# The depthwise convolution's multiply moved from GpSimd to ScalarE in a one-core two-layer kernel

## What is computed

```python
u = a * jax.nn.sigmoid(ag)
u = jnp.pad(u, ((0, 0), (CONV_KSIZE - 1, 0), (0, 0)))
u = lax.conv_general_dilated(u, conv_w, (1,), 'VALID', dimension_numbers=('NWC', 'WIO', 'NWC'),
                             feature_group_count=CONV_WIDTH) + conv_b
u = jax.nn.silu(layer_norm(u, conv_ln_g, conv_ln_b))
```

## Time and profile before

| | |
|---|---|
| median of 3 runs | 2055.93 us (2053.12 to 2060.07) |
| profiled execution, its own time | 2055.43 us |
| its span | 2053.8 us |
| PE busy | 1906.3 us (93%) |
| DVE, ACT, POOL busy | 852.5, 585.5, 690.9 us |
| NSA units | from about 1270 to 1461 us of the span |

### The profile page before, as it was taken

The page is one execution under the profiler, slowest core; times in us unless marked ns, Lnnn a source line. Parts: engine busy times, 40 slices in busy tenths (PEclk is TensorE's granted clock), DMA queues, the critical chain, the costliest instruction groups (busy, mean ns, idle before and its releaser), DMA issues.

```text
span 2053.8 us, 23262 instructions
## 1 busy us (share of the span) xinstructions
PE 1906.3 (93%) x8758; PEld 1383.8 (67%) x8758; DVE 852.5 (42%) x1252; ACT 585.5 (29%) x1074; POOL 690.9 (34%) x396
## 2 busy tenths in 40 slices
PE   5999979999986899999779898999997989999999
PEld 3888757767866444444258776677675858888887
DVE  4221666645723122313253365667636643312331
ACT  2323334442221101110033223545444212222221
POOL 4444324332410000000022334776762424444442
PEclk9999989999995999999988999999998989999999
DMA  5222212242410577778832423121234412232231
GB/s 195 95 83 93 82 57 77 87 154 67 135 41 1 197 256 284 284 269 297 336 134 85 131 81 103 64 76 62 67 113 156 140 64 93 93 102 93 93 101 43
DMA packets 79301, 255.86 MB, mean 125 GB/s; under 512 B 8800, under 2 KB 9824, under 8 KB 79200
## 3 DMA queue, kind: packets, MB, share of 16 engines
q1 hardware_dynamic: 61632, 222.33, 31.5%
q10 hardware_dynamic: 17568, 32.11, 4.4%
HBM read 239.73 MB, written 14.68 MB: 124 GB/s over the span
## 4 chain that ended last, share of the span: by engine, by line
PE 85%; DVE 8%; DMA 3%; ACT 2%; issue 1%; ACTq 1%; SPq 0%; POOL 0%; DVEq 0%
PE psum L493 83%; DMA ring<-stream 2%; DVE root L1628 1%; DVE area_r L1610 1%; PE psum L1059 1%; DVE area L1617 1%; DVE area L1644 1%; DVE area L1697 1%; DVE root L1615 1%; ACTq L1547 1%; PE psum L584 1%; DVE area L2072 1%; ACT root L1191 1%; PE psum L749 0%; DMA area<-xT 0%
## 5 line engine op out<-in xcount | busy, mean ns | idle before, releaser
L493 PE MATMUL psum<-area_r,ring_hi 128*128 128x512 f32 (+1 forms) x3168 | 1004.4, 399 | 20.3 <-DVE area_r L1610 13.6
L413 POOL TENSOR_TENSOR ring_lo<-ring,ring_hi 128x1024 fp32r<-128x1024 f32 x220 | 533.0, 2426 | 1325.3 <-ACT ring_hi L1191 1325.3
L493 PEld LDWEIGHTS psum<-area_r,ring_hi 128*128 128x128 f32 x3168 | 596.1, 191 | 164.4 <-issue 26.4
L493 PE MATMUL psum<-area_r,ring_lo 128*128 128x512 f32 (+1 forms) x1584 | 622.3, 393 | 0.0
L1191 ACT ACTIVATE ring_hi<-ring 128x1024 fp32r<-128x1024 f32 x220 | 232.0, 1057 | 633.4 <-PE psum L493 604.6
L493 PEld LDWEIGHTS psum<-area_r,ring_lo 128*128 128x128 f32 x1584 | 302.9, 191 | 63.6
L493 PE MATMUL psum<-ring,area 128*64 128x512 f32 x768 | 195.4, 618 | 19.0 <-DMA ring<-stream 17.7
L1191 ACT ACTIVATE area<-psum 128x512 f32<-128x512 f32 (+3 forms) x248 | 119.8, 510 | 257.7 <-PE psum L493 143.4
L1628 DVE RECIPROCAL root<-root 128x512 f32<-128x512 f32 (+1 forms) x30 | 94.1, 3138 | 138.1 <-ACT root L1191 138.1
L493 PE MATMUL psum<-area 128*64 128x128 f32 (+6 forms) x832 | 112.1, 346 | 14.2 <-DVE area L1629 9.7
L493 PE MATMUL psum<-ring_hi,area_r 128*128 128x512 f32 (+1 forms) x352 | 107.6, 387 | 15.9 <-DVE area_r L1610 15.8
(11 more groups left out here) (193 smaller groups left out, 1641.9 us busy)
## 6 DMA issues: line engine op xcount, KB each, us to landing
ring<-stream SPq DMA_DIRECT2D x420, 512.0 KB, 3.5
area<-gates ACTq DMA_DIRECT2D x40, 256.0 KB, 5.9
gates<-root ACTq DMA_DIRECT2D x24, 256.0 KB, 2.0
gates<-area ACTq DMA_DIRECT2D x16, 256.0 KB, 3.5
area<-xT SPq DMA_DIRECT2D x8, 256.0 KB, 8.1
area<-xT ACTq DMA_DIRECT2D x8, 256.0 KB, 3.3
x_kept<-area ACTq DMA_DIRECT2D x8, 256.0 KB, 5.8
area<-x_kept ACTq DMA_DIRECT2D x8, 256.0 KB, 3.9
```

Of the source, the lines that this page charges most:

```text
L413: nc.gpsimd.tensor_tensor(ring_lo[:, c % RS, :], ring[:, c % R, :], ring_hi[:, c % RS, :].bitcast(F32), ALU.subtract).then_inc(w_lo, 1)
L493: return nc.tensor.matmul(out, lhsT, rhs, start=first, stop=last)
```

## The change

ScalarE makes the multiplies of GpSimd's 60 two-instruction steps, each as an activation `Copy` with the weight as a per-partition scale, into the same two scratch tiles. GpSimd keeps the add, and now takes four steps ahead of each `low`. In unit u ScalarE makes terms 4u+2 and 4u+3 between `gate2_out` and the four exponentials, and terms 4u+4 and 4u+5 behind the two small exponentials. Each term from the fifth step on first waits until GpSimd's add of step s-2, the last to read this scratch tile, is done.

```diff
@@ conv_step (GpSimd)
-                    term = tile(KVC + s % 2)
                     pool.wait_ge(S("conv_pool"), s - 1)
-                    link(nc.gpsimd.tensor_scalar(term, src, w, 0.0, ALU.mult, ALU.add))
-                    ins = nc.gpsimd.tensor_tensor(tile(CV + c), tile(CV + c), term, ALU.add)
+                    pool.wait_ge(S("conv_term"), s - 1)
+                    ins = nc.gpsimd.tensor_tensor(tile(CV + c), tile(CV + c), tile(KVC + s % 2), ALU.add)
                 ins.then_inc(S("conv_pool"), 1)
 
             for n in range(3 * KD):
-                for s in range(3 * n, min(3 * n + 3, 2 * TAPS)):
+                for s in range(4 * n, min(4 * n + 4, 2 * TAPS)):
                     conv_step(s)
@@ ScalarE
+            def conv_term(lo, hi):
+
+                for s in range(lo, min(hi, 2 * TAPS)):
+                    tap, c = divmod(s, 2)
+                    if s >= 4:
+                        act.wait_ge(S("conv_pool"), s - 1)
+                    A(tile(KVC + s % 2), upad[:, 2 + c, tap:tap + T], ACT.Copy, 0.0,
+                      par("convw", (2 + c) * TAPS + tap)).then_inc(S("conv_term"), 1)
@@ the loop over NSA units (ScalarE), behind gate2_out(u - 1), ahead of the four exponentials
                 if u < len(NSA_UNITS):
+                    if u == 0:
+                        act.wait_ge(S("conv_u"), CONVT)
+                        act.wait_ge(S("kv_xp"), 8)
+                    conv_term(2 + 4 * u, 4 + 4 * u)
                     n = P * (NSA_UNITS[u][1] + 1)
@@ the same loop, behind the two small exponentials
+                    conv_term(4 + 4 * u, 6 + 4 * u)
```

More of the change, by code:

```diff
@@ L238, in block_program @@
                      "vsw_out", "gn_mm", "gn_act", "kv_raw", "kv_x2", "kv_xp", "cmp_gelu", "cmp_mm", "cmp_out", "cmp_root",
-                     "conv_sig", "conv_out", "conv_pool", "on_rec", "on_bc", "on_norm", "ya_split", "conv_u", "ln_sum", "ln_d", "ln_sq", "ln_root", "ln_n", "ln_out",
+                     "conv_sig", "conv_out", "conv_pool", "conv_term", "on_rec", "on_bc", "on_norm", "ya_split", "conv_u", "ln_sum", "ln_d", "ln_sq", "ln_root", "ln_n", "ln_out",
                      "g2_in0", "g2_in1", "g2_in2", "g2_in3", "g2_act", "g2_out", "x3_out", "ff_silu", "ff_out", "fin", "xf_out", "br_split", "x_spilled", "g2_on", "stored"):
```

## The result

The changed kernel takes 2082.74 us (median of 4 runs, 2077.27 to 2088.63) against 2054.52 for the kernel before: a ratio of 1.0131, 95% interval 1.0105 to 1.0157. It is slower by 28.2 us between the medians; 2087 us was forecast from a base of 2055.9, that is 31 us more.

The account below looks back on a forecast made before the run. TensorE was taken to set the period; exponentials waiting for terms were to add 23.2 us and clock falls 7.8, together 31.0 on 2055.43 us: 2086.4, given as 2087 us. The range was 2066 to 2102 us.

Parts of the forecast that it names:

- Place and cause: Ahead of the exponentials, ScalarE's two front terms wait for GpSimd's adds behind low, delaying TensorE: +23.2 us.
- H: The end of a unit's ring_hi copy, where one NSA unit is cut from the next; GpSimd's low waits for it.
- One premise: In a unit, TensorE depends on fresh ScalarE work only at nsa_cscores, which needs the first two exponentials.
- C: The start of nsa_cscores in a unit; TensorE was said to have fixed work from there to the next H.
- The chain from H: In a unit: low, two GpSimd adds, signal and second term put the first exponential at H + 5.67 us.
- C minus H: Time from H to C in a unit: 6.53 to 7.17 us forecast by width, adding 23.2 us in all.
- VectorE's relief: GpSimd's shorter work leaves VectorE's L1697 and L1644 undisturbed; unit 15 gains 1.33 us, elsewhere exponentials wait for terms.
- "faster" rival: Relief counts, the wait doesn't: waits of 7.1 us and a 2.6 us clock fall go, 2046 us; chance 0.06.
- unit 2's wait: TensorE's 3.12 us wait in unit 2 before the change, laid to GpSimd holding up VectorE; the faster case removes it.
- The clock: TensorE's new waits halve its clock in units 1, 6, 10, 14, less unit 2's fall: 3 x 2.6 = 7.8 us.
- the middle terms: The two terms behind the small exponentials on ScalarE, forecast free in time; uncovered, up to 18 us in all.
- the stage: The stretch from C of unit 0 to C of unit 15, 176.2 us before the change and 204.1 after.

Follow-up runs that it names:

- e1_shift: Changed kernel, but GpSimd takes steps 4n+2 to 4n+5 ahead of each low (six ahead of the first); ratio 0.9986 against the kernel before.
- e2_four: Changed kernel with four scratch tiles for the terms instead of two, GpSimd's order kept; ratio 0.9999 against the kernel before.
- e6_one_column: Changed kernel with the two front terms of units 1 to 14 made for one column only, waits kept; one run, 2077.61 us.
- e3_behind: Changed kernel with the two front terms put behind the four exponentials; ratio 0.9979 against the kernel before.
- e4_no_terms: Changed kernel without ScalarE's terms and the waits for them, GpSimd keeping only its adds; ratio 0.9990 against the kernel before.
- e7_fill: Changed kernel with eight unused TensorE matmuls ahead of nsa_cscores in units 1, 2, 6, 10 and 14; ratio 1.0134 against the kernel before.
- e5_mul4: Kernel before the change with four GpSimd steps ahead of each low, multiplies left on GpSimd; ratio 1.0061 against the kernel before.

## Why the prediction held

- **Place and cause.** Right: the waits for GpSimd's steps 4u and 4u+1 behind `low`. e1_shift, e2_four and e6_one_column separate the wait from ScalarE's work: the exponentials start at H + 1.1 to 1.8 with the work and without the wait (e1_shift, from unit 2 on), and at H + 5.2 with the wait and nearly without the work. One premise is too narrow: `nsa_cscores` is the only point at which TensorE depends on ScalarE as long as the copies of transposes are early; in e3_behind they are not, and unit 1 loses 1.8 us behind C.
- **The chain from H.** Forecast H + 5.67 for the first exponential, measured 5.58 to 5.61. The term takes 0.72 us; I had 0.71, between rows with no and with two per-partition operands. C minus H was forecast as 6.53, 6.74, 6.96, 7.17 and is 6.44, 6.65, 6.86, 7.07: 0.1 us too much a unit, 21.8 and not 23.2 us in all.
- **VectorE's relief.** Right in the changed kernel: L1710 takes 1.38 us in unit 9, and unit 15 has no wait. Right also that it pays nothing while the exponentials wait for the terms. But the size of the "faster" rival, 10 us, was too large: e4_no_terms has the relief alone and gives 3.5 us. The step that failed was to let unit 2's wait go altogether; adds in a row held VectorE there as well (3.58 us with adds alone, 3.12 with the multiplies between). SBUF — State Buffer (the Trainium skill, section "SBUF: two separate sides") has it that the shared port is locked for a whole instruction and not divided. The run agrees as far as it goes: beside GpSimd's adds, which have nothing shorter between them, VectorE's two steps took 3.52 us and not 1.41.
- **The clock.** Forecast: falls in units 1, 6, 10 and 14 and one fewer in unit 2, 7.8 us. Measured: all four, but unit 2's stayed, and a fall costs 2.4 us in unit 1 and 1.6 in the others, not 2.6. Together 6.1 us. The cost of 2.6 was read from a single fall; by the stretches of 1 us it had half the clock for about 6.8 us, as unit 1 has now, and those of units 2, 6, 10 and 14 last about 3.4 us. Two errors partly cancel, one fall too few and each too dear, so that the clock's term came within 1.7 us is in part luck. That the length of a wait tells where the clock falls was wrong as well, as the last section shows.
- **What should cost nothing.** Right: the middle terms (C to next H is unchanged in all units without a fall, 7.09, 6.25, 6.64) and the memory attention (8.12 us a gate tile). The stretch behind unit 15 kept its length to 0.1 us; the 5.3 us ahead of unit 0 are not the change's. The sum of 31.0 us answers to the stage's 27.9; the 28.2 between the medians carry the noise of the other stages.

## What to carry to other kernels

When work moves to another engine, price the wait that it brings and not only its duration: find what the awaited instruction stands behind on its own queue, and what stands behind the waiter. Here 1.3 us of activations were free and the same two, waiting for an add behind a `low`, cost 28 us; one line that moved two adds to the other side of the `low` gave them back. And an engine that is idle for a quarter of each unit, as GpSimd was, isn't worth relieving for itself: its gain has to be looked for in those it holds up, unit by unit.

## What the runs showed that was not expected

A wait of TensorE of 1.86 us (unit 8) left the clock at full speed in the changed kernel; one of 1.85 us (unit 4 of e7_fill) was followed by half speed when other waits had been filled with matmuls. In e6_one_column, waits of 2.35 us (units 6, 10 and 14) had no fall behind them and one of 1.85 us (unit 2) had. In e5_mul4 the same unit shape gives it both ways: units 10 and 14, TensorE's timeline and one stretch of 1 us behind each wait.

```profile
1408.92 0.41 PE L493 MATMUL psum<-kc,area 64*128 64x31 f32 x4 [2.28 <-ACT area L1190]
...
1459.15 0.41 PE L493 MATMUL psum<-kc,area 64*128 64x31 f32 x4 [2.30 <-ACT area L1190]
```

```profile
1411.00:1412.00 1.00, 1.00 (x5) 0.50 0.00 0
...
1461.00:1462.00 1.00, 1.00 (x8) 1.00 0.00 0
```

C to the next H is 7.80 us in unit 10 and 6.20 in unit 14, and unit 2 of that run has a wait of 2.83 us and no fall. So the length of a single wait does not decide, and a filled wait can move a fall to another one. What does decide is open; no run here tells. The time over all moves by some 10 us from run to run through stages far from the change, so of a change worth 0.1 to 0.3% the stage's length in the trace says more than twelve timed runs.
